# Inverse of the delta rule's matrix in six doublings of 64-column products, with conditioning rows between them and one gate tile ahead of it

## What is computed

```python
# conditioning: six rows of 1024, in three groups of 2048 values
mod = silu(c) @ w_ada[l] + b_ada[l]
shift1, scale1, gate1, shift2, scale2, gate2 = jnp.split(mod, 6, axis=-1)
# gated delta rule: chunks of 64 tokens, 4 heads of 128
a_low = jnp.where(strict, jnp.einsum('bnhie,bnhje->bnhij', kb, kc) * decay, 0.0)
lhs = a_low + jnp.eye(C)
u = lax.linalg.triangular_solve(lhs, vb, left_side=True, lower=True)
w = lax.linalg.triangular_solve(lhs, kb * jnp.exp(gc)[..., None], left_side=True, lower=True)
...                                   # scan over the chunks: states and outputs o
o = rms_norm(o, dn_norm_w) * jax.nn.silu(dz)     # dz: the gate, one of the input projections
```

## Time and profile before

| | |
|---|---|
| median of three runs | 2144.7 us (2143.56 to 2146.27) |
| the profiled execution | 2143.65 us, of which the profile's span is 2141.7 us |
| TensorE busy | 2074.2 us, 97% of the span |
| VectorE, ScalarE, GpSimd busy | 978.9, 327.8, 50.3 us |
| mean granted TensorE clock | 0.996 of 2.4 GHz |
| DMA | 593.52 MB, mean 277 GB/s |

### The profile page before, as it was taken

One profiled execution on the slowest core, in us unless ns is written; L12 is line 12 of the kernel. 1 busy time (PEld: TensorE's weight loads), 2 busy tenths in 40 slices (PEclk: granted clock), 3 DMA queues, 4 the chain that ended last, 5 costly groups with the idle time before them and its releaser, 6 DMA issues.

```text
span 2141.7 us, 24148 instructions
## 1 busy us (share of the span) xinstructions
PE 2074.2 (97%) x9716; PEld 1143.4 (53%) x9722; DVE 978.9 (46%) x1574; ACT 327.8 (15%) x729; POOL 50.3 (2%) x30
## 2 busy tenths in 40 slices
PE   6999999999999999999999999999999999999999
PEld 4858533333333333333333457868884658868874
DVE  1486444333333333333332256734676167626684
ACT  1142100000010000000000113302110113311110
POOL 0001000000000000000000002000000011000000
PEclk9999999999999999999999999999999999999999
DMA  9559389999999999999999834334442634334441
GB/s 371 218 195 365 113 359 417 427 428 428 428 428 426 428 428 427 429 426 429 427 428 427 307 133 158 139 105 157 146 145 97 224 121 158 110 126 155 148 157 51
DMA packets 133443, 593.52 MB, mean 277 GB/s; under 512 B 9774, under 2 KB 66270, under 8 KB 105178
## 3 DMA queue, kind: packets, MB, share of 16 engines
q1 hardware_dynamic: 133338, 592.02, 69.7%
HBM read 590.91 MB, written 3.18 MB: 277 GB/s over the span
## 4 chain that ended last, share of the span: by engine, by line
PE 81%; DMA 11%; DVE 5%; issue 1%; ACT 1%; POOL 1%; SPq 0%; POOLq 0%; DVEq 0%
PE bank L1624 24%; PE bank L679 22%; DMA ring<-in_w_dram 10%; PE bank L689 8%; PE bank L2751 6%; PE bank L2714 3%; PE bank L1765 2%; PE bank L1605 2%; PE bank L2729 2%; PE bank L962 2%; PE bank L3106 1%; PE bank L1641 1%; DMA ring<-in_w_ada_dram 1%; DVE arena L1289 1%; PE bank L593 1%
## 5 line engine op out<-in xcount | busy, mean ns | idle before, releaser
L1624 PE MATMUL bank<-ring,arena 128*64 128x512 f32 x2304 | 509.7, 594 | 11.4 <-DMA ring<-in_w_dram 9.9
L679 PE MATMUL bank<-wide,ring 128*128 128x256 f32 x2368 | 517.2, 381 | 2.8 <-ACT wide L2983 2.6
L679 PEld LDWEIGHTS bank<-wide,ring 128*128 128x128 f32 x2368 | 451.0, 191 | 67.5 <-issue 5.9
L1624 PEld LDWEIGHTS bank<-ring,arena 128*64 128x64 f32 x2304 | 161.1, 137 | 350.0 <-issue 322.4
L1265 DVE TENSOR_SCALAR arena<-bank 128x512 f32<-128x512 f32 x32 | 22.1, 692 | 376.3 <-PE bank L1624 376.3
L689 PE MATMUL bank<-ring,wide 128*128 128x512 f32 (+2 forms) x384 | 151.4, 554 | 0.0
L2411 DVE SCALAR_TENSOR_TENSOR arena<-bank,arena 128x254 f32<-128x254 f32 (+1 forms) x176 | 76.7, 477 | 84.3 <-ACT arena L2555 82.7
L689 PEld LDWEIGHTS bank<-ring,wide 128*128 128x128 f32 x384 | 72.6, 190 | 74.6 <-issue 71.3
L1269 DVE RECIPROCAL arena<-arena 128x512 f32<-128x512 f32 x32 | 107.3, 3353 | 1.1
L1441 ACT ACTIVATE arena<-arena 128x512 f32<-128x512 f32 x32 | 20.2, 631 | 492.9 <-DVE arena L1265 492.9
L1624 PE MATMUL bank<-wide,arena 128*64 128x512 f32 x392 | 89.0, 595 | 0.7 <-ACT arena L1445 0.7
(11 more groups left out here) (515 smaller groups left out, 1949.6 us busy)
## 6 DMA issues: line engine op xcount, KB each, us to landing
ring<-in_w_dram SPq DMA_DIRECT2D x144, 2048.0 KB, 24.1
wide<-in_w_dram SPq DMA_DIRECT2D x24, 2048.0 KB, 24.9
arena<-in_w_dram SPq DMA_DIRECT2D x22, 2048.0 KB, 27.0
ring<-in_w_up_dram SPq DMA_DIRECT2D x44, 1024.0 KB, 6.8
ring<-in_w_in_dram SPq DMA_DIRECT2D x21, 2048.0 KB, 8.1
ring<-in_w_ada_dram SPq DMA_DIRECT2D x12, 2048.0 KB, 9.0
ring<-in_w_down_dram SPq DMA_DIRECT2D x10, 2048.0 KB, 7.7
ring<-in_w_out_dram SPq DMA_DIRECT2D x6, 2048.0 KB, 8.4
```

The lines of the kernel that those rows point to most:

```text
L679: ins = pe.matmul(B.bank(name, j)[:, i * T:(i + 1) * T], w[:, k, (first + i) * P:(first + i + 1) * P], hT[:, k, :], start=(k == 0), stop=( ...
L1624: ins = pe.matmul(bank[g * SLOTS:(g + 1) * SLOTS, :], lhsT, rhs[:, g * CH:(g + 1) * CH], start=start, stop=stop)
```

## The change

1. **Inverse.** The blocks of 8 with their squares go. The start is now blocks of 2, written by masks (`pairs`: minus the neighbour entry plus the identity, for Xm and for XTm), and six levels (`LEVELS`) join blocks of 2, 4, ... 64. At each level a product takes only the columns that can change (`level(..., odd)`), 64 of 128, and `half4` puts four of them into half a bank; ACT and DVE move 128x256 instead of 128x512. T1 lies in zeroed areas (GpSimd memsets). Xm is a tile of its own, so that A needs no longer to be overwritten. BT has two buffers, so GpSimd makes it two levels ahead.
2. **Conditioning rows.** The third group's bias matmuls stand before the first level, and its eight pieces of four matmuls (`ada_row`) between the products of the levels 0 to 3, one behind `bx` and one behind the first tile's `xl`. Its bank is kept out of the rotation (`add_beside`).
3. **Gate.** The first tile of z stays where both were; the second (`zrow_t(pe, 1)`) now stands behind the transposes of A, directly in front of the inverse. The DVE work for the first tile stands between the two attention results, that for the second behind the last level.
4. **Scalings on ACT.** v times beta happens as ACT moves v out of the banks (eight 128x128 pieces); KBG and Kdec are twelve 128x128 ACT copies with a scale, before the inverse. DVE did these (L835, L838, L840).
5. **Loads.** The slot of z is free later, so the load into it (the third group's a=1) goes behind the two of the output projection. `spread(2)` waits for `u1` as well, since the tile that it fills now holds v. `layer_params` stands behind `dno`. The masks in the constants are others (three 128-column masks more in all), in two loads.

```diff
 def delta_v:
+            def pairs(dst, src, mask, odd):
+                one, where_ = everywhere(level(ident, -1, odd), 8), everywhere(level(c(mask), -1, odd), 8)
+                d, s_ = level8(dst, odd), level8(src, odd)
+                v.scalar_tensor_tensor(out=d, in0=s_, scalar=-1.0, in1=where_, op0=ALU.mult, op1=ALU.mult)\
+                 .then_inc(S["e_mat"], 1)
+                v.wait_ge(S["e_mat"], 2 * odd + 1)
+                v.tensor_tensor(d, d, one, ALU.add).then_inc(S["e_mat"], 1)
...
-            for nm, last in (("zz", None), ("xx", "zz")):
-                for n, j in enumerate(XJOBS):
-                    update(nm, n, j, ALU.add, (last, n) if last else None)
...
+            for lv in range(LEVELS):
+                for n, j in enumerate(XJOBS if lv < LEVELS - 1 else XJOBS[1::2]):
+                    m = tile_level((Xm, XTm)[j // 2], j % 2, lv, j // 2)
+                    if lv:
+                        v.wait_ge(*B.taken(f"xl{lv - 1}", n if lv < LEVELS - 1 else 2 * n + 1))
+                    v.wait_ge(*B.ready(f"xl{lv}", n))
+                    v.tensor_tensor(m, m, narrow(half4(f"xl{lv}", n), lv), ALU.subtract).then_inc(B.free(f"xl{lv}", n), 1)
+            z_silu_v(v, then, 1)
 def delta_t:
-            ada_rows_t(pe, 2)
...
+            zrow_t(pe, 1)
+            pe.wait_ge(S["e_mat"], 4)
...
+            def half_product(lhsT, rhs, lv, odd):
+                return lambda out, u: pe.matmul(out.rearrange("p (b r) -> p b r", r=2 << lv), lhsT[:, u, :],
+                                                level(rhs[:, u, :], lv, odd), start=True, stop=True)
+            pe.wait_ge(*B.room("ag2"))
+            ada_row(pe, 2, None)
+            third = [(a, k) for a in (0, 2, 3, 1) for k in range(2)]
+            for lv in range(LEVELS):
+                t1, last = T1[lv], lv == LEVELS - 1
                 pe.wait_ge(S["bmat"], lv + 1)
...
+                for tt in range(2):
+                    if lv:
+                        pe.wait_ge(*B.taken(f"xl{lv - 1}", 2 * tt))
+                    half(f"bx{lv}", tt, half_product(BT[lv % 2], Xm, lv, 0), tt)
+                if lv < 4:
+                    ada_row(pe, 2, third[2 * lv])
+                for tt in range(2):
+                    pe.wait_ge(*B.taken(f"bx{lv}", tt))
+                    if lv:
+                        pe.wait_ge(*B.taken(f"xl{lv - 1}", 2 * tt + 1))
+                    if not last:
+                        half(f"xl{lv}", 2 * tt, half_product(XTm, t1, lv, 0), tt)
+                    half(f"xl{lv}", tt if last else 2 * tt + 1, half_product(t1, XTm, lv, 1), tt)
+                    if tt == 0 and lv < 4:
+                        ins = ada_row(pe, 2, third[2 * lv + 1])
...
 sync:
+            last_in = ada_at[2] + 1
+            for n in [n for n in range(N1) if n != last_in] + [last_in]:
...
+                    sp.wait_ge(S["dno"], 1)
                     layer_params(sp, 0, late=False)
-                    sp.wait_ge(S["dno"], 1)
 vector:
             result_v(v, then, B, S, jobs1[0], 0, att[:, 0, :], den[0], flag="attn_p")
+            v.wait_ge(S["gexp"], 1)
+            v.tensor_tensor(bg, beta, egc, ALU.mult).then_inc(S["vb"], 1)
+            z_silu_v(v, then, 0)
             result_v(v, then, B, S, jobs1[1], 1, att[:, 1, :], den[1], flag="attn_p")
 tensor:
-            rows_of("z", n + 2)
+            zrow_t(pe, 0)
             ada_rows_t(pe, 1)
```

More of the change, by code:

```diff
@@ L76, in add, with add_beside @@
         for _ in range(count):
+            b = self.n % 8
+            self.n += 1
+            self.bank.append(b)
+            self.nth.append(self.used[b])
+            self.used[b] += 1
+    def add_beside(self, name, count, kept):
+        self.at[name] = len(self.bank)
+        for _ in range(count):
+            if self.n % 8 == kept:
+                self.n += 1
             b = self.n % 8
@@ L137, in constants @@
     parts["early"] = -BIG * (f < p)
-    parts["blk8"] = (p // 8 == f // 8)
-    for lv in range(4):
-        L = 8 << lv
-        parts[f"low{lv}"] = (p // (2 * L) == f // (2 * L)) & ((f // L) % 2 == 1) & ((p // L) % 2 == 0)
+    masks = {}
+    for lv in range(-1, LEVELS):
+        L = 2 << lv if lv >= 0 else 1
+        masks[f"low{lv}"] = (p // (2 * L) == f // (2 * L)) & ((f // L) % 2 == 1) & ((p // L) % 2 == 0)
+    for lv in range(3, LEVELS):
+        parts[f"low{lv}"] = masks[f"low{lv}"]
     for qt in range(TT):
@@ L169, in constants @@
     parts["bucket"] = (np.arange(P)[:, None] == bucket[None, :])
+    parts["pair"], parts["pairT"] = masks["low-1"], masks["low-1"].T
+    for lv in range(3):
+        parts[f"low{lv}"] = masks[f"low{lv}"]
     where, at, cols = {}, 0, []
@@ L502, in ada_rows_t, with ada_row @@
             ins.then_inc(B.full(f"ag{g}"), 1)
+        def ada_row(pe, g, piece):
+            rows = B.bank(f"ag{g}")
+            if piece is not None:
+                a, k = piece
+                w, landed = w1_slot(ada_at[g] + a)
+                pe.wait_ge(*landed)
+            for i in range(4):
+                j = 4 * g + i
+                if piece is None:
+                    ins = pe.matmul(rows[32 * i:32 * i + 32, :], ident[0:12, j:j + 1].to_broadcast([12, 32]), badr[0:12, :],
+                                    start=True, stop=False)
+                else:
+                    ins = pe.matmul(rows[32 * i:32 * i + 32, :], silu_c[:, 2 * a + k, :], split(w, 2)[:, k, i * CH:(i + 1) * CH],
+                                    start=False, stop=(piece == (1, 1)))
+            return ins
         def ada_rows_s(act, g):
@@ L720, in b4, with half4, level @@
             return split(B.bank(name, i)[:], 4)
+        def half4(name, i):
+            return split(B.bank(name, i)[:, 0:2 * P], 4)
         XJOBS = (0, 2, 1, 3)
-        def delta_pool(pool):
-            for lv in range(4):
-                if lv:
-                    pool.wait_ge(*B.ready(f"bx{lv - 1}", 1))
-                else:
-                    pool.wait_ge(*B.ready("xx", 0))
-                    pool.wait_ge(*B.taken("aT", 1))
-                pool.tensor_tensor(BT, AT, everywhere(c(f"low{lv}"), 8), ALU.mult).then_inc(S["bmat"], 1)
+        def level(m, lv, odd):
+            if lv < 0:
+                return m.rearrange("p (b two) -> p b two", two=2)[:, :, odd]
+            L = 2 << lv
+            return m.rearrange("p (b two r) -> p b two r", two=2, r=L)[:, :, odd, :]
@@ L794, in delta_v @@
                 ins.then_inc(B.free("kk", tt), 1)
+            def pairs(dst, src, mask, odd):
[5 more added lines that the diff above has]
+                v.tensor_tensor(d, d, one, ALU.add).then_inc(S["e_mat"], 1)
+            for tt in range(TT):
+                v.wait_ge(*B.taken("kk", tt))
+            v.wait_ge(S["unit"], 1)
+            pairs(Xm, Am, "pairT", 0)
             for tt in range(TT):
@@ L3016, in _ @@
             exps_s(act, S, 1, 1, AHD ** -0.5, expo[1], amax[1], den[1])
-            for j in range(TT):
-                act.wait_ge(*B.ready("z", j))
-                act.activation(dz[:, j, :], B.bank("z", j)[:], ACT.Copy).then_inc(B.free("z", j), 1)
+            zrow_s(act, 0)
             ada_rows_s(act, 1)
@@ L3022, in _ @@
             decays_s(act)
-            for j in range(TT):
-                act.wait_ge(*B.taken("z", j))
-                act.activation(normw[0][:, j * DW:(j + 1) * DW], dz[:, j, :], ACT.Exp, scale=-1.0).then_inc(S["zx"], 1)
             features_s(act)
```

218 lines of the change are left out of this document (119 added, 99 removed), and 3 rows, old and new, of the table p.

## The result

| | before | changed |
|---|---|---|
| median | 2145.64 us (20 executions, 2143.56 to 2148.05) | 2149.94 us (20 executions; 19 of them 2146.82 to 2153.74) |
| ratio | | 1.0020, 95% interval 1.0014 to 1.0027 |
| profiled execution | 2143.65 us | 2152.66 us, span 2150.9 us, mean clock 0.993 |

A forecast was written before the change was run, and what follows sets the result against it. Experts are transfer-bound, so the mixer's TensorE chain shifts everything one for one. Gate 6.9, group 7.99, fours 30.4, wait 0.7, switches 0.5: 46.5 against 43.80, starting 5.2 earlier; forecast 2.6 less, 2142.1, range 2140.5 to 2143.8.

The forecast's parts named there:

- Of the 6.9, 1.7 are lost in a longer wait there: With the 6.9 us gate tile moved, TensorE starts the second values only 5.2 earlier, losing 1.7 waiting for ACT.
- clock rival: In the inverse's levels, streaming 64 columns lowers TensorE's clock: 10 us lost, 2152; chance 0.08.
- DVE's chain up to the scaled k ends at 149.62 + 1.22 = 150.84 whatever TensorE does: Ahead of the decay rows: DVE's scaling of k takes 1.22, so the rows start at about 151.27 instead of 156.49.
- the price of the masks: Before the inverse: DVE's four 128x512 passes take about 0.69 each, over by 170.5, 3.6 before TensorE wants them.
- the term for switches: Conditioning pieces standing alone between full-array products: changes of shape cost 0.5 us in all.
- fours of 0.893: In the inverse: four 64-column products cost 0.893, as with 128 columns; 34 fours take 30.4 us against 32.1.
- more gain: Rival in the levels: products go by their columns, 2128, or weaker, kept waits go, 2140; chance 0.15, full form 0.04.
- the wait ahead of `u0`: End of the inverse: one wait of 0.7 us, where it was 0.90 before.
- levels with no wait: New inverse levels: ACT, DVE and GpSimd work is covered, so no wait; at the other end 0.24 each, 1.4 more.
- the gate 6.97: Second gate tile, moved in front of the inverse: 6.9 us of TensorE there, 0 by itself.
- The biases: Expert bias loads ahead of the output projection: land at 241.6, 3.7 behind their start; hidden by 1.0.
- SP queue: Rival: parameter loads slow by themselves, biases land at 255.9, output projection late on DVE: 9 lost, 2151; chance 0.07.

The follow-up runs named there:

- e1: Changed kernel with bf16 filler matmuls in TensorE's three waits ahead of the second tile's values: 2146.13 us, ratio 1.0000 against the kernel before.
- e8: e3 with the gate's second tile right behind the second tile's values and the changed kernel's load order: 2148.61 us, ratio 1.0012 against the kernel before.
- e6: e3 with the gate's second tile directly ahead of the values, the unit matrix later and the changed kernel's load order: 2139.14 us, ratio 0.9971.
- e4: Changed kernel with the third conditioning group in one block behind the gate's second tile: 2149.89 us, ratio 1.0017 against the kernel before.
- e3: Only the new inverse and what it needs; gate tiles and load order as before, conditioning group one block ahead of the levels: 2141.06 us, ratio 0.9977.
- e2: Changed kernel with GpSimd making the unit matrix only after the decay rows: 2146.44 us, ratio 1.0002 against the kernel before.
- e10: e2 with its two TensorE waits ahead of the values filled with bf16 matmuls: 2145.28 us, ratio 1.0001 against the kernel before.
- e9: Changed kernel run again with nothing edited, for a second trace: 2151.65 us, ratio 1.0025 against the kernel before.
- e5: e3 with GpSimd's first two BT products waiting until DVE's masks are done: 2141.67 us, ratio 0.9977 against the kernel before.
- e7: e3 with the three expert bias loads issued ahead of the ten parameter loads: 2140.76 us, ratio 0.9973 against the kernel before.

## Why the prediction was wrong

**The step that failed** is "Of the 6.9, 1.7 are lost in a longer wait there". It priced a wait of TensorE at its own length, saw one wait where there were three, and put the clock behind them at nothing. The trace after has 3.4 us of waits in the 8 us ahead of the values, where before had little but the 0.80, and behind them the clock falls: 4.8 in the first trace, 3.2 in the second. e1 takes the falls away by filling the waits, e8 brings the first one by moving the gate (with its order of loads, which e6 clears). The Trainium skill (TensorE: Matmul & The Clock Gate, Why this matters for your kernels) warns of a long idle gap between bursts of matmuls. Here no single gap was above 1.52, and the traces of the changed kernel, of e4 and of e8 show the fall behind three short ones.

**The clock rival was in the list, at the wrong place.** I had it inside the inverse ("in levels 4 and 5 alone", or "in all six"), for their 64 columns, with 0.08. Its sign and size (2152, against 2149.94) came close to the result by luck: its mechanism is refuted by e3. The place to look was the row that I had read: a wait that grows from 0.80 to 1.7, among short jobs.

**1.1 at the start**: "DVE's chain up to the scaled k ends at 149.62 + 1.22 = 150.84 whatever TensorE does". It does not depend on TensorE, but on GpSimd, whose unit matrix moved into it. The Trainium skill (SBUF — State Buffer, SBUF: two separate sides) calls the port pair of the two an exclusive lock. The trace agrees: GpSimd's product ends at 151.16, 1.83 after DVE's begins, and 1.83 + 1.22 = 3.05 is near the 2.92 measured. The contention is worth 1.9 (e2); the forecast had the values 0.5 later behind the transposes of q and k than e2 shows, and that hid a part of it. The same mistake stands in the price of the masks, "about 0.69 each" and "over by 170.5": the last two took 2.62 and 2.72 and ended at 179.80, 1.3 before TensorE wanted them instead of 3.6, which still cost nothing. I had read what each engine has to do, not what runs beside it.

**1.8 in the stretch**: the term for switches, 0.5 in all, was 2.2. A piece among products costs 0.27 more than in a block (e4), eight of them 2.2. The end of the last level up to `u0` is 0.1 longer than summed. The rest of the sum held: fours of 0.893 also at 64 strided columns (5.36 for six in e3), so neither form of "more gain" came; the wait ahead of `u0` 0.63; levels with no wait; the gate 6.97.

**The biases** came at 254.63, not 241.6. 9.4 of that is `dno` being later (the parameters start at 241.69 instead of 232.3), nearly all the rest a landing of 7.1 (issued at 247.51) instead of 3.7. Yet the rival "SP queue" cost nothing that the traces show. TensorE was late as well, so DVE began its first bank at 256.34, only 2.6 behind the 253.7 at which TensorE had it ready (234.31 plus the 19.40 of before, 227.50 to 246.90). DVE then catches up in three banks and waits 2.05 for the last one, as it did before, 2.10. The forecast's cover, 1.0, ended at the first bank; only the rival's sum had some catching up in it, and put it too low.

**Summed**: forecast -2.5 at `u0`, plus 1.1, 4.8 and 1.8 is +5.2, as measured (221.40 against 216.20). Without the falls the kernel equals before (e1 1.0000; e10, without the contention too, 1.0001).

**Open** is what makes the second fall at 222, which one of two traces has, and how often the first comes in e2. Open too is how much of a fall is owed to the waits and how much to the thin work between them: before the change, the clock falls at 126 behind 8-column matmuls with no wait at all. The runs show that with this thin work the three waits bring the fall and that without them it stays away; they do not show that waits of this length would do it between dense matmuls. That the medians mix executions with and without such falls is argued from the mean clocks (0.993 in the slowest of e2 and e9, 0.996 or 0.997 in the quickest), not shown in a trace of each.

## What to carry to other kernels

A job that TensorE does early, with slack behind it, may be what keeps its clock up: before moving it, add up all the waits that open in its old place, and price them with some of the work behind them at half the clock (3.2 to 4.9 us here), not by their length alone. Better, put the moved job into the largest wait (e6). And when DVE's chain leads, look at what GpSimd does in the same microseconds.

## What the runs showed of the hardware

- Waits of 1.2 (0.8 in e4), 0.7 and 1.5 us among transposes and 64-column products were followed by 7 to 10 us at 1.2 GHz (changed kernel twice, e4, e8); 0.22 and 1.52 were not in one trace (e2); 0.80 alone was not (e3), nor 0.66 (e6).
- 16 strided products of 64 columns, each with weights of its own, take 3.57 us (e3), 0.223 each, which is what products of 128 columns take.
- Four matmuls of 32 by 512 side by side, standing between full-array products, cost 0.27 us more than in a row of their kind (changed kernel, e4).
- DVE's pass over two SBUF tiles took 2.92 instead of 1.22 (changed kernel, e2), or 2.76 instead of 0.69 (e3, e5), beside a GpSimd product.
- Small loads issued 16 us behind 8 MB on the same queue came 12.2 us after their issue (e7), with a DMA share of 1.01 from 230 to 242; before the change, with the DMA engines idle ahead of them (share 0.01 from 216 to 230), it was 3.7 us.
